# The expert stage's gated sum: rows weighed before they are stored, and added in memory by the store

## The chip, the cores and the metric

The kernel runs on one core of a Trainium2 chip. The metric is device time in microseconds (us) of that core; less is better. Before the change it is 2638.87 us, the median of three runs (2636.39 to 2640.18).

## The reference

Two transformer blocks on 1024 tokens of 1024 features. The change touches the last part of the second block only, the mixture of experts and the last norm:

```python
def hierarchical_moe(xn, w_rg, b_rg, w_re, b_re, w1, w3, w2):
    # xt: 1024 tokens x 1024; 4 groups of 8 experts, top-1 group, top-2 experts in it
    gate = p_g * jax.nn.softmax(top_v, axis=-1)              # 2 gates a token
    expert = g_idx[:, None] * EXPERTS_PER_GROUP + top_i      # 2 experts a token
    # assignments sorted by expert, padded to blocks of MOE_BLOCK = 128 rows of one expert
    def block_ffn(args):
        tok, e = args
        xb = xt[tok]
        hb = jax.nn.silu(xb @ w1[e]) * (xb @ w3[e])          # 1024 -> 512
        return hb @ w2[e]                                    # 512 -> 1024
    y = jnp.einsum('nk,nkd->nd', gate, y_assign)             # weigh and add the two rows of a token
    return y

x = x + hierarchical_moe(rmsnorm_2(x, norm_moe_g), ...)
return rmsnorm_2(x, norm_f_g)
```

All of it is in float32. A token has two expert outputs; each is weighed by its gate and both are added to the residual row, and the row is then normalised.

## The kernel before

The stages up to the router are unchanged. The last call of `project_out` writes the residual rows (x3, 1024 rows of 4 KB in memory) and the normalised rows (xn), and computes the router's logits.

`route` (line 2260) runs mostly on VectorE (DVE). It finds the two experts and the two gates of each token (lines 2372 and 2373: an SBUF table `gates` of 128 partitions by 2 by 8) and the tables of slots. A block is 128 slots of one expert; every expert has one block (its first 128 assignments), and a 33rd block and a loop for further blocks take what is over. A slot is a partition. `slot_token` says which token a slot holds, `slot_row` says which row of the 2048 rows of y_rows its output goes to (token, plus 1024 for the second choice). Slots are filled from the first partition on; the entry of an empty slot is beyond the bounds check, and the indirect DMA leaves it out.

`experts` (line 2484) runs the 33 blocks. Every engine walks through the same list `steps()`: for block b the two halves of w1, the turned h of block b-1, the two halves of w3, the turned x of block b+1, the two halves of w2 of block b-1.

- SyncE (SP) loads the weights of block b+2 (`ExpertWeights.load`, line 2463): w1, w3 and w2 are 2 MB each, as 128 partitions of 16 KB, in two buffers each. Each load waits until DVE has finished with the raw weights of two blocks ago. SP issues in program order. Since w2 of a block is used about one block later than its w1 and w3, the load of w2 waits longest, and w1 and w3 of the next block go out right behind it: one burst of 6 MB a block.
- ScalarE (ACT) rounds each half matrix to w_hi (line 2735), DVE computes the rest w_lo (line 2796); a ring of four halves feeds TensorE (PE), which does three products for one (lines 2660, 2666, 274 to 276).
- GpSimd (POOL) issues two indirect DMAs a block: `gather_rows` (line 2435) fetches 128 rows of xn into ex_x, and `scatter` (line 2597) stores ex_y to y_rows. The first may run when x of two blocks before is turned, the second when ACT has copied the block's output out of PSUM (line 2755, ex_y<-ex_py), in two buffers.
- During the last block SP also loads the eight tiles of residual rows (line 2579).

`combine` (line 2850) begins when all scatters have landed. SP loads the eight y tiles of the first choice (line 2864), ACT the eight of the second (line 2872). For each tile of 128 tokens DVE multiplies and adds twice (2888, 2890), ACT takes the sum of squares and the root (2876, 2877), DVE the reciprocal and the norm (2896, 2897), and SP stores the tile (2867). DVE runs the adds of the next tile ahead of the norm of this one.

All DMA queues, whichever engine issues, share the same 16 DMA engines. In the profile q1 is SP's queue, q0 POOL's and q10 ACT's.

Of the kernel before, what the change touches and what calls it, by code (L numbers as in the profile page):

```python
# [27 lines left out]
P = 128  # L28
# [2231 lines left out]
def route(c, expert_weights, pl, bias, gates, slot_token, slot_row, extra_expert, n_rest, xg):  # L2260
# [7 lines left out]
    with ExitStack() as s:  # L2268
        def sb(name, shape, dt=F32):
            return s.enter_context(nc.sbuf_tensor(f"rt_{name}", shape, dt))  # L2270
# [19 lines left out]
        none, row = sb("none", [P, NBLK]), sb("row", [P, NBLK])  # L2290
        slots, filled = c.sem("rt_slots"), c.sem("rt_filled")
# [45 lines left out]
        def route_dve(dve):  # L2337
# [35 lines left out]
            step(V.tensor_tensor(gates[:, 1, :], gates[:, 0, :], v2[:, :], ALU.mult))  # L2373

# [48 lines left out]
            step(V.scalar_tensor_tensor(slot_row[:, :], pt[:, 0:NBLK], -1.0, row[:, :], ALU.add, ALU.add))  # L2423
            step(V.tensor_tensor(cmp[:, :, :], pend[:, :].unsqueeze(1).to_broadcast([P, NEXTRA, NE]),
# [6 lines left out]
        return route_sp, route_pool, route_pe, route_act, route_dve  # L2431
# [52 lines left out]
def experts(c, weights, xn, y_rows, slot_token, slot_row, n_rest, xg, x3, tail, gates, out, routing):  # L2484
# [32 lines left out]
    x, _, gain, x_in, gain_in = tail  # L2517
    route_sp, route_pool, route_pe, route_act, route_dve = routing
    x_t = x3.rearrange("(t p) d -> t p d", p=P)

    with ExitStack() as s:
# [7 lines left out]
        idx = sb("idx", [P, LINE], I32)  # L2529
        xT_hi, xT_lo = sb("xT_hi", [P, D], F32R), sb("xT_lo", [P, D], F32R)  # L2530
# [9 lines left out]
        combine_sp, combine_act, combine_dve = combine(c, s, tail, y_rows, gates, out, y[:, 0, :])  # L2540
# [22 lines left out]
        with nc.Block() as block:  # L2563
            @block.sync
            def _(sp):
                route_sp(sp)

                for b in range(2, NB):
                    weights.load(sp, b, up_lo, down_lo)

                def load(i):
                    e = sp.value_load(weights.extra_expert[0:1, bass.ds(i + 1, 1)], min_val=0, max_val=NE - 1)
                    sp.wait_ge(r_free, i + 1)
                    for m, w in (("w1", weights.w1), ("w3", weights.w3), ("w2", weights.w2)):
# [12 lines left out]
            def _(pool):  # L2587
                route_pool(pool)

                def gather(b):  # L2590
                    if b >= 2:
                        pool.wait_ge(x_turned, b - 1)
                    gather_rows(nc, xg, xn, slot_token, b, g_in[b % 2])

                def scatter(b):
                    pool.wait_ge(y_ready, b + 1)
                    nc.gpsimd.indirect_dma_start(y_rows, bass.IndirectOffsetOnAxis(slot_row[:, b:b + 1].bitcast(U32), 0),
                                                 y[:, b % 2, :], None, bounds_check=2 * S - 1, oob_is_err=False
                                                 ).then_inc(y_out[b % 2], 16)

                gather(0)
                gather(1)
                gather(2)
                for n, m, b, half in steps():
                    if m == "turn_x" and b + 2 < NB:
                        gather(b + 2)
                    if m == "w1" and half == 1 and b >= 2:
                        scatter(b - 2)
                scatter(NB - 2)
                scatter(NB - 1)  # L2610

                def regather(i):
                    pool.wait_ge(r_free, i + 1)
                    nc.gpsimd.tensor_copy(idx[:, 0:1], slot_token[:, bass.ds(i + NB, 1)])
                    nc.gpsimd.tensor_copy(idx[:, 1:2], slot_row[:, bass.ds(i + NB, 1)]).then_inc(r_idx, 1)
                    pool.wait_ge(r_idx, i + 1)
                    pool.sem_inc(r_gathers, 1)
                    nc.gpsimd.indirect_dma_start(xg[:, 0, :], None, xn,
                                                 bass.IndirectOffsetOnAxis(idx[:, 0:1].bitcast(U32), 0),
                                                 bounds_check=S - 1, oob_is_err=False).then_inc(r_x_in, 16)  # L2620
                    pool.wait_ge(r_y_ready, i + 1)
                    pool.sem_inc(r_gathers, 1)
                    nc.gpsimd.indirect_dma_start(y_rows, bass.IndirectOffsetOnAxis(idx[:, 1:2].bitcast(U32), 0),
                                                 y[:, 0, :], None, bounds_check=2 * S - 1, oob_is_err=False
                                                 ).then_inc(r_y_out, 16)
# [100 lines left out]
            def _(act):  # L2726
# [24 lines left out]
                def store(b, n):  # L2751
# [3 lines left out]
                    nc.scalar.activation(y[:, b % 2, :], p_y[:, :], ACT.Copy).then_inc(y_ready, 1)  # L2755
# [18 lines left out]
                def block_of_rest(i):  # L2774
# [4 lines left out]
                    nc.scalar.activation(y[:, 0, :], p_y[:, :], ACT.Copy).then_inc(r_y_ready, 1)  # L2779
# [60 lines left out]
def combine_buffers(c, weights, xg):  # L2840

    x = [w[1][:, t * D:(t + 1) * D] for w in (weights.w1s, weights.w3s) for t in range(NT // 2)]
    y = [w[0][:, t * D:(t + 1) * D] for w in (weights.w1s, weights.w3s, weights.w2s) for t in range(NT // 2)]
    y += [weights.w2s[1][:, t * D:(t + 1) * D] for t in (1, 2)] + [xg[:, t, :] for t in range(2)]
    return x, y, weights.w2s[1][:, 0:D], [c.sem(f"cb_x_in{t}") for t in range(NT)], c.sem("cb_gain_in")


def combine(c, stack, tail, y_rows, gates, out, sq):  # L2850


    nc, io = c.nc, c.io
    x, y, gain, x_in, gain_in = tail
# [3 lines left out]
    eps_ready, added, rms_ready, ready = (c.sem(f"cb_{n}") for n in ("eps", "added", "rms", "ready"))  # L2858
    y_in = [c.sem(f"cb_y_in{t}") for t in range(NT)]
    out_done = c.sem("cb_out_done")  # L2860

    def combine_sp(sp):
        for t in range(NT):
            sp.dma_start(y[2 * t], y_rows[t * P:(t + 1) * P, :]).then_inc(y_in[t], 16)
# [5 lines left out]
    def combine_act(act):  # L2870
        for t in range(NT):
            act.dma_start(y[2 * t + 1], y_rows[S + t * P:S + (t + 1) * P, :]).then_inc(y_in[t], 16)
        act.wait_ge(eps_ready, 1)
        for t in range(NT):
            act.wait_ge(added, t + 1)
# [4 lines left out]
    def combine_dve(dve):  # L2880
        nc.vector.memset(eps[:, :], EPS).then_inc(eps_ready, 1)
        dve.wait_ge(gain_in, 16)

        def add(t):
            xx = x[t]
            dve.wait_ge(x_in[t], 16)
            dve.wait_ge(y_in[t], 32)
# [5 lines left out]
        def norm(t):  # L2893
            xx = x[t]
            dve.wait_ge(rms_ready, t + 1)
            c.vstep(dve, nc.vector.reciprocal(ss[:, 2, t:t + 1], ss[:, 1, t:t + 1]))
            nc.vector.scalar_tensor_tensor(xx, xx, ss[:, 2, t:t + 1], gain, ALU.mult, ALU.mult
                                           ).then_inc(ready, 1)

        for t in range(NT):  # L2900
            add(t)
            if t >= 1:
                norm(t - 1)
        norm(NT - 1)
# [18 lines left out]
def build(nc, io):  # L2923
# [4 lines left out]
    x1, x2, x3, xn = (scratch(f"{n}_rows", S) for n in ("x1", "x2", "x3", "xn"))  # L2928
    og, yb, y_rows = scratch("og_rows", S), scratch("yb_rows", S), scratch("y_rows", 2 * S)
# [6 lines left out]
    with ExitStack() as ctx:  # L2936
# [8 lines left out]
        with ExitStack() as late:  # L2945
            with ExitStack() as front:
# [56 lines left out]
                bias = late.enter_context(nc.sbuf_tensor("rt_bias", [P, LINE], F32))[:, 0:NG + NE]  # L3003
# [8 lines left out]
            routing = route(c, expert_weights, logits, bias, gates, slot_token, slot_row, extra_expert, n_rest, xg)  # L3012
            tail = combine_buffers(c, expert_weights, xg)
            experts(c, expert_weights, xn, y_rows, slot_token, slot_row, n_rest, xg, x3, tail, gates, io["out"], routing)


# [16 lines left out]
```

## Time and profile before

| | us |
|---|---|
| median of three runs | 2638.87 |
| the profiled execution's own time | 2638.07 |
| its span, first to last instruction | 2636.3 |
| PE busy | 2483.1 (94%) |
| DVE busy | 1255.8 (48%) |
| ACT busy | 1140.5 (43%) |
| POOL busy | 598.1 (23%) |
| DMA moved | 434.78 MB, 165 GB/s on average |

The busy shares are averages over stages with quite different loads. The page also cuts the span into 40 equal slices, a digit a slice: the busy share in tenths of each engine and, in the line DMA, of the 16 DMA engines. The expert stage is the last quarter of the span. "Landing" is the time from the issue of a DMA until its semaphore has counted it as complete. The idle time of an engine is told with the instruction whose end released it.

### The profile page before, as it was taken

The numbers are of one execution on the slowest core, as the hardware profiler recorded it, in microseconds if no ns is written. First come the engines' busy times: TensorE is split into PE (matmuls) and PEld (weight loads), VectorE is DVE, ScalarE is ACT, GpSimd is POOL, SyncE is SP. The second block draws the span as 40 slices with busy tenths as digits, with TensorE's granted clock in tenths as the row PEclk, the third lists the DMA queues.
The fourth block names the chain that finished last, engine by engine and source line by source line (L and its number), as shares of the span: only waits on it lengthen the run. The fifth ranks groups of instructions, "written<-read, shape, count | busy, mean of one in ns | idle before, by whom it ended". The sixth has DMA issues, their size and how long they took to land. (4 is left out here: it accounts for less than half of the span.)

```text
span 2636.3 us, 30070 instructions
## 1 busy us (share of the span) xinstructions
PE 2483.1 (94%) x11958; PEld 1999.5 (76%) x11958; DVE 1255.8 (48%) x1583; ACT 1140.5 (43%) x1612; POOL 598.1 (23%) x497
## 2 busy tenths in 40 slices
PE   7999998889999999999999999999987999999992
PEld 6888874447787888878887877885775888888882
DVE  6420205553304121125543853006128898888886
ACT  4212225553332122214232742235225878877883
POOL 0312302213222122332220751254110111111100
PEclk9999999999999999999999999999987999999996
DMA  4322121203311131132424732441446999999996
GB/s 171 110 66 92 48 77 52 81 9 128 120 37 60 33 117 60 56 117 69 128 64 165 279 131 81 143 160 65 132 178 255 379 382 391 393 385 383 390 363 246
DMA packets 146581, 434.78 MB, mean 165 GB/s; under 512 B 16232, under 2 KB 66632, under 8 KB 133768
## 3 DMA queue, kind: packets, MB, share of 16 engines
q1 hardware_dynamic: 95536, 374.23, 37.6%
q10 hardware_dynamic: 38120, 31.50, 3.6%
q0 software_dynamic: 12784, 27.11, 2.9%
q8 instruction: 96, 1.57, 0.2%
q14 instruction: 45, 0.37, 0.0%
HBM read 377.70 MB, written 72.91 MB: 171 GB/s over the span
## 5 line engine op out<-in xcount | busy, mean ns | idle before, releaser
L2796 DVE TENSOR_TENSOR ex_w_lo<-ex_w,ex_w_hi 128x2048 fp32r<-128x2048 f32 x198 | 447.9, 2290 | 62.0 <-ACT ex_w_hi L2735 61.2
L2735 ACT ACTIVATE ex_w_hi<-ex_w 128x2048 fp32r<-128x2048 f32 x198 | 377.0, 1916 | 20.3 <-PE ex_pb L2666 11.0
L221 POOL TENSOR_TENSOR p_w_lo<-w_raw,p_w_hi 128x512 fp32r<-128x512 f32 (+1 forms) x146 | 191.5, 1345 | 627.1 <-ACT p_w_hi L249 594.9
L221 POOL TENSOR_TENSOR p_w_lo_rest<-w_raw,p_w_hi_rest 128x512 fp32r<-128x512 f32 x88 | 118.0, 1375 | 254.4 <-ACT p_w_hi_rest L249 254.4
L846 DVE CUSTOM_DVE_ANT_0 att_sc<-att_ps_s,logc 128x128 f32<-128x128 f32 (+7 forms) x96 | 71.7, 752 | 120.8 <-PE att_ps_s L781 120.4
L274 PE MATMUL p_ps<-p_w_hi,hT_hi 128*128 128x512 f32 (+1 forms) x320 | 120.9, 378 | 0.0
L276 PE MATMUL p_ps<-p_w_hi,hT_lo 128*128 128x512 f32 (+1 forms) x320 | 118.5, 370 | 0.0
L275 PE MATMUL p_ps<-p_w_lo,hT_hi 128*128 128x512 f32 (+1 forms) x320 | 118.0, 369 | 0.0
L249 ACT ACTIVATE p_w_hi<-w_raw 128x512 fp32r<-128x512 f32 (+1 forms) x133 | 74.7, 600 | 88.9 <-PE mix_ps_rest L276 49.3
L2435 POOL DMA_INDIRECT ex_x<-xn_rows,slot_token x33 | 35.5, 1075 | 338.1 <-PE ex_px L2640 315.7
L274 PE MATMUL ex_py<-ex_w_hi,ex_hT_hi 128*128 128x512 f32 x264 | 105.6, 400 | 1.9 <-DVE ex_hT_lo L2805 1.9
L274 PE MATMUL o_ps<-o_w_hi,o_m_hi 128*128 128x512 f32 x256 | 102.1, 399 | 5.0 <-DVE split_cols L1165 5.0
L2660 PE MATMUL ex_pa<-ex_w_hi,ex_xT_hi 128*128 128x512 f32 x264 | 103.9, 394 | 2.4 <-ACT ex_xT_hi L2739 1.2
L2660 PE MATMUL ex_pb<-ex_w_hi,ex_xT_hi 128*128 128x512 f32 x264 | 105.8, 401 | 0.0
L2660 PE MATMUL ex_pa<-ex_w_lo,ex_xT_hi 128*128 128x512 f32 x264 | 103.6, 392 | 0.0
L2660 PE MATMUL ex_pb<-ex_w_lo,ex_xT_hi 128*128 128x512 f32 x264 | 103.3, 391 | 0.0
L276 PE MATMUL ex_py<-ex_w_hi,ex_hT_lo 128*128 128x512 f32 x264 | 103.1, 391 | 0.0
L275 PE MATMUL ex_py<-ex_w_lo,ex_hT_hi 128*128 128x512 f32 x264 | 103.0, 390 | 0.0
L276 PE MATMUL o_ps<-o_w_hi,split_cols 128*128 128x512 f32 x256 | 101.1, 395 | 0.0
L275 PE MATMUL o_ps<-o_w_lo,o_m_hi 128*128 128x512 f32 x256 | 101.0, 395 | 0.0
L1053 POOL TENSOR_TENSOR split_cols<-plain_cols,o_m_hi 128x1024 fp32r<-128x1024 f32 x20 | 48.0, 2401 | 195.6 <-ACT o_m_hi L1116 195.6
L274 PE MATMUL p_ps<-hT_hi,p_w_hi 128*128 128x512 f32 x224 | 87.3, 390 | 0.2 <-POOL p_w_lo L221 0.2
(507 smaller groups left out, 6249.2 us busy)
## 6 DMA issues: line engine op xcount, KB each, us to landing
ex_w<-w SPq DMA_DIRECT2D x99, 2048.0 KB, 14.4
w_raw<-w_in SPq DMA_DIRECT2D x42, 1024.0 KB, 5.1
w_raw<-w_out SPq DMA_DIRECT2D x8, 1024.0 KB, 8.2
x_rows<-o_x SPq DMA_DIRECT2D x16, 512.0 KB, 2.6
qk_columns<-ml_qk_first ACTq DMA_DIRECT2D x16, 512.0 KB, 3.2
w_raw<-w_xkv SPq DMA_DIRECT2D x8, 1024.0 KB, 6.1
plain_cols<-x SPq DMA_DIRECT2D x8, 512.0 KB, 8.7
w_raw<-w_in SPq DMA_DIRECT2D x16, 256.0 KB, 4.0
```

Of the source, the lines that this page charges most:

```text
L221: emit(self.lo(n)[:, 0:w], self.half(n // (KC // 2), w)[:, n % (KC // 2), :], self.hi(n)[:, 0:w].bitcast(F32), ALU.subtract).then_inc(self ...
L249: copy = lambda out, in_: self.c.nc.scalar.activation(out, in_, ACT.Copy)
L274: pe.matmul(out, a, x, start=start, stop=False)
L275: pe.matmul(out, a, y, start=False, stop=False)
L276: return pe.matmul(out, b, x, start=False, stop=stop)
L846: nc.vector.tensor_tensor_reduce(row_of(i, k), bank_of(i, k), logc[:, S - (a + 1) * P:S], -SCALE, -NEG, ALU.add, ALU.min, nmx[:, 2 * i + k ...
L1053: nc.gpsimd.tensor_tensor(tile(cols, t), tile(plain, t), m_hi[:, t % 2, :, :].bitcast(F32), ALU.subtract).then_inc(rest, 1)
L2435: nc.gpsimd.indirect_dma_start(xg[:, b % 2, :], None, xn, bass.IndirectOffsetOnAxis(slot_token[:, b:b + 1].bitcast(U32), 0), bounds_check= ...
L2660: pe.matmul(ps[:, :], xT_hi[:, k * P:(k + 1) * P], w[:, n % RING, at], start=(k == 0 and w is w_hi), stop=False)
L2735: nc.scalar.activation(w_hi[:, n % RING, :], raw_half(n), ACT.Copy).then_inc(hi_done, 1)
L2796: nc.vector.tensor_tensor(w_lo[:, n % RING, :], raw_half(n), w_hi[:, n % RING, :].bitcast(F32), ALU.subtract).then_inc(down_lo if m == "w2 ...
```

## The change

The two weighed outputs of a token are no longer stored apart and combined at the end. The residual rows and the result of the experts share one memory tensor `sums` of 1024 + 128 rows (`x3` is its first 1024 rows). In each block ACT multiplies the output rows by the slots' gates while it copies them out of PSUM, and the scatter adds them to the rows of `sums` in memory (`compute_op=ALU.add`). For that:

- SP writes the gates once to a memory table `gate_rows` of 2048 words, and POOL gathers the 128 gates of each block from it by an indirect DMA of one word a slot, with `slot_row` as index.
- a new table `slot_sum` holds the row of `sums` for each slot: the token, or for an empty slot a spare row of its own partition, 1024 + p. So the scatter now has 128 valid rows always. Two DVE instructions more in `route` make it, and one makes `spare_row`.
- a scatter waits until the scatter before it has landed, since both may add to the same row.
- `combine` loads eight tiles of `sums`, four by SP and four by ACT, and has the norm alone; DVE's adds, the sixteen y loads and the eight x loads in the last block are gone.

```diff
 (route)
+            V.tensor_scalar(spare_row[:, :], c.const("tokid")[:, 0:1], float(S), None, ALU.add).then_inc(gates_ready, 1)
...
+            step(V.scalar_tensor_tensor(row[:, :], pt[:, 0:NBLK], -1.0, none[:, :], ALU.add, ALU.add))
+            V.tensor_scalar(slot_sum[:, 0:NBLK], row[:, :], spare_row[:, :], None, ALU.min).then_inc(rows_known, 1)
 (experts, SP)
                 route_sp(sp)
+                sp.wait_ge(gates_ready, 1)
+                with nc.allow_non_contiguous_dma(reason="one gate a token, once"):
+                    sp.dma_start(gate_rows.rearrange("(k t p) o -> p (k t) o", k=2, p=P),
+                                 gates[:, :, :].rearrange("p k t -> p (k t)").unsqueeze(2)).then_inc(gates_out, 16)
...
-                for t in range(NT):
-                    sp.wait_ge(up_lo, 4 * NE - (2 if t < NT // 2 else 0))
-                    sp.dma_start(x[t], x_t[t]).then_inc(x_in[t], 16)
 (experts, POOL)
+                def gather_gates(b):
+                    if b == 0:
+                        pool.wait_ge(gates_out, 16)
+                        pool.wait_ge(rows_known, 1)
+                    if b >= 2:
+                        pool.wait_ge(y_ready, b - 1)
+                    nc.gpsimd.indirect_dma_start(slot_gate[:, b % 2:b % 2 + 1], None, gate_rows,
+                                                 bass.IndirectOffsetOnAxis(slot_row[:, b:b + 1].bitcast(U32), 0),
+                                                 bounds_check=2 * S - 1, oob_is_err=False).then_inc(gate_in[b % 2], 16)
                 def scatter(b):
                     pool.wait_ge(y_ready, b + 1)
-                    nc.gpsimd.indirect_dma_start(y_rows, bass.IndirectOffsetOnAxis(slot_row[:, b:b + 1].bitcast(U32), 0),
-                                                 y[:, b % 2, :], None, bounds_check=2 * S - 1, oob_is_err=False
-                                                 ).then_inc(y_out[b % 2], 16)
+                    if b >= 1:
+                        pool.wait_ge(y_out[(b - 1) % 2], 16 * ((b - 1) // 2 + 1))
+                    nc.gpsimd.indirect_dma_start(sums, bass.IndirectOffsetOnAxis(slot_sum[:, b:b + 1].bitcast(U32), 0),
+                                                 y[:, b % 2, :], None, bounds_check=S + P - 1, oob_is_err=True,
+                                                 compute_op=ALU.add).then_inc(y_out[b % 2], 16)
...
                         scatter(b - 2)
+                        gather_gates(b)
 (experts, ACT, store)
-                    nc.scalar.activation(y[:, b % 2, :], p_y[:, :], ACT.Copy).then_inc(y_ready, 1)
+                    act.wait_ge(gate_in[b % 2], 16 * (b // 2) + 16)
+                    nc.scalar.activation(y[:, b % 2, :], p_y[:, :], ACT.Copy, scale=slot_gate[:, b % 2:b % 2 + 1]
+                                         ).then_inc(y_ready, 1)
 (combine)
-        for t in range(NT):
-            sp.dma_start(y[2 * t], y_rows[t * P:(t + 1) * P, :]).then_inc(y_in[t], 16)
+        for t in range(0, NT, 2):
+            load(sp, t)          # x[t] <- sums[t * P:(t + 1) * P, :]
...
-        for t in range(NT):
-            act.dma_start(y[2 * t + 1], y_rows[S + t * P:S + (t + 1) * P, :]).then_inc(y_in[t], 16)
+        for t in range(1, NT, 2):
+            load(act, t)
...
-            c.vstep(dve, nc.vector.scalar_tensor_tensor(xx, y[2 * t], gates[:, 0, t:t + 1], xx,
-                                                        ALU.mult, ALU.add))
-            nc.vector.scalar_tensor_tensor(xx, y[2 * t + 1], gates[:, 1, t:t + 1], xx, ALU.mult, ALU.add
-                                           ).then_inc(added, 1)
```

The loop for further blocks is changed in the same way.

POOL's order at the start of the expert stage before (ex_x is the gathered input, ex_y the output of a block):

```order
L2435 DMA ex_x<-xn_rows,slot_token 128x1024 [waits att_turned,o1_g_in]
L2435 DMA ex_x<-xn_rows,slot_token 128x1024
L2435 DMA ex_x<-xn_rows,slot_token 128x1024 [waits ex_x_turned] x3
L2597 DMA y_rows<-ex_y,slot_row 2048x1024 [waits ex_y_ready]
L2435 DMA ex_x<-xn_rows,slot_token 128x1024 [waits ex_x_turned]
L2597 DMA y_rows<-ex_y,slot_row 2048x1024 [waits ex_y_ready]
L2435 DMA ex_x<-xn_rows,slot_token 128x1024 [waits ex_x_turned]
L2597 DMA y_rows<-ex_y,slot_row 2048x1024 [waits ex_y_ready]
```

And with the change (ex_idx holds the gathered gates, rt_bias the table slot_sum):

```order
L2439 DMA ex_x<-xn_rows,slot_token 128x1024 [waits att_kept1,o1_x_in1]
L2439 DMA ex_x<-xn_rows,slot_token 128x1024
L2608 DMA ex_idx<-gate_rows,slot_row 128x1 [waits att_kept0,o2_post]
L2608 DMA ex_idx<-gate_rows,slot_row 128x1
L2439 DMA ex_x<-xn_rows,slot_token 128x1024 [waits o2_h_hi] x3
L2616 DMA sums_rows<-ex_y,rt_bias 1152x1024 [waits ex_y_ready]
L2608 DMA ex_idx<-gate_rows,slot_row 128x1 [waits ex_y_ready]
L2439 DMA ex_x<-xn_rows,slot_token 128x1024 [waits o2_h_hi]
L2616 DMA sums_rows<-ex_y,rt_bias 1152x1024 [waits ml_m_ready,ex_y_ready]
L2608 DMA ex_idx<-gate_rows,slot_row 128x1 [waits ex_y_ready]
L2439 DMA ex_x<-xn_rows,slot_token 128x1024 [waits o2_h_hi]
```

Two gate gathers stand before the third x gather, and from then on each block has three transfers: the adding scatter, the gate gather of the block two later, the x gather.

DVE's order at the end of the program before (ex_w and ex_x are the buffers of the tiles, cb_ss the sums of squares):

```order
L2881 MEMSET cb_eps 128x1
L2888 SCALAR_TENSOR_TENSOR ex_w_1<-ex_w_0,gates,ex_w_1 128x1024
L2890 SCALAR_TENSOR_TENSOR ex_w_1<-ex_w_0,gates,ex_w_1 128x1024
L2888 SCALAR_TENSOR_TENSOR ex_w_1<-ex_w_0,gates,ex_w_1 128x1024
L2890 SCALAR_TENSOR_TENSOR ex_w_1<-ex_w_0,gates,ex_w_1 128x1024
L2896 RECIPROCAL cb_ss<-cb_ss 128x1
L2897 SCALAR_TENSOR_TENSOR ex_w_1<-ex_w_1,cb_ss 128x1024
L2888 SCALAR_TENSOR_TENSOR ex_w_1<-ex_w_0,gates,ex_w_1 128x1024
L2890 SCALAR_TENSOR_TENSOR ex_w_1<-ex_w_0,gates,ex_w_1 128x1024
```

And with the change:

```order
L2913 MEMSET cb_eps 128x1
L2917 RECIPROCAL cb_ss<-cb_ss 128x1
L2918 SCALAR_TENSOR_TENSOR ex_w_0<-ex_w_0,cb_ss,ex_w_1 128x1024
L2917 RECIPROCAL cb_ss<-cb_ss 128x1
L2918 SCALAR_TENSOR_TENSOR ex_w_0<-ex_w_0,cb_ss,ex_w_1 128x1024
```

The two multiply-and-add instructions of each tile are gone, and reciprocal and norm follow each other tile by tile.

## Rows read from the trace of the kernel before

**Rows 1.** The page: span, engines and the span in 40 slices.
```profile
span 2636.3 us, 30070 instructions
...
PE   7999998889999999999999999999987999999992
...
DMA  4322121203311131132424732441446999999996
```

**Rows 2.** Windows of 100 us in the expert stage: busy us of each engine.
```profile
core 0: us, PE busy (x) PEld busy (x) DVE busy (x) ACT busy (x) POOL busy (x), PEclk, DMA share, GB/s
...
2200.00:2300.00 100.00, 100.00 (x475) 83.83 (x474) 89.79 (x52) 80.32 (x57) 12.26 (x11) 1.00 0.96 389
2300.00:2400.00 100.00, 100.00 (x473) 83.81 (x472) 89.27 (x51) 80.74 (x57) 11.58 (x11) 1.00 0.96 393
```

**Rows 3.** The chain of waits, one expert block: start us, us, what.
```profile
2123.02 1.81 PE ex_pa L2660 x8
...
2140.77 1.81 PE ex_pa L2660 x8
```

**Rows 4.** Weight loads: who waited for line 2474 and its landing; 2477's landing; line 2481.
```profile
  ACT ex_w_hi L2735: 4.9, 6
...
DMA to landing us min/median/max: 8.2/14.4/16.3
...
DMA to landing us min/median/max: 7.8/19.5/21.3
...
L2481 SPq DMA_DIRECT2D ex_w<-w x33: 327/328/529, 1968.7 to 2559.8; - x33
...
DMA to landing us min/median/max: 7.7/8.7/22.5
```

**Rows 5.** Fine windows around the next burst's issue, columns as in rows 2.
```profile
2208.23:2210.01 1.78, 1.78 (x9) 1.50 (x8) 1.62 (x2) 1.78 (x2) 0.00 (x0) 1.00 1.05 433
...
2222.25:2223.00 0.75, 0.75 (x5) 0.62 (x4) 0.73 (x2) 0.22 (x1) 0.00 (x0) 1.00 0.49 208
```

**Rows 6.** DMA queues between 2060 and 2540 us: packets, MB, share of 16 engines.
```profile
DMA packets 19523, 185.06 MB, mean 386 GB/s; under 512 B 5626, under 2 KB 5626, under 8 KB 9092
...
q1 hardware_dynamic: 11703, 170.50, 87.0%
q0 software_dynamic: 7795, 14.21, 7.7%
```

**Rows 7.** Idle of ACT before line 2755 (us, times); line 2597's durations, starts and landing.
```profile
  PE ex_py L276: 33.1, 33
...
L2597 POOL DMA_INDIRECT y_rows<-ex_y,slot_row x33: 974/1009/1291, 2036.1 to 2593.6; - x33
...
DMA to landing us min/median/max: 2.6/10.9/12.1
```

**Rows 8.** Timeline of the start: start us, us, instruction, idle before it.
```profile
1993.00 0.21 DVE L2423 SCALAR_TENSOR_TENSOR slot_row<-rt_pt,rt_row 128x48 int32<-128x48 f32 x1
...
2000.95 1.00 POOL L2435 DMA_INDIRECT ex_x<-xn_rows,slot_token  x1 [4.75 <-PE ex_px L2640]
```

**Rows 9.** Timeline of the end, columns as in rows 8.
```profile
2596.28 3.57 SPq L2864 DMA_DIRECT2D ex_w<-y_rows  x7
...
2601.16 1.28 DVE L2888 SCALAR_TENSOR_TENSOR ex_w<-ex_w,gates,ex_w 128x1024 f32<-128x1024 f32 x1 [12.13 <-DMA ex_w<-y_rows]
...
2603.86 1.06 ACT L2876 ACTIVATE ex_y<-ex_w 128x1024 f32<-128x1024 f32 x1 [11.02 <-DVE ex_w L2890]
...
2606.85 1.28 DVE L2897 SCALAR_TENSOR_TENSOR ex_w<-ex_w,cb_ss 128x1024 f32<-128x1024 f32 x1
2607.62 0.19 ACT L2876 ACTIVATION_READ_ACCUMULATOR ex_y<-ex_w 128x1 f32 x1
2607.84 0.29 ACT L2877 ACTIVATE cb_ss<-cb_ss,cb_eps 128x1 f32<-128x1 f32 x1
...
2631.94 1.28 DVE L2897 SCALAR_TENSOR_TENSOR ex_w<-ex_w,cb_ss 128x1024 f32<-128x1024 f32 x1
```

More of the change, by code:

```diff
@@ L2257, in load_router, with route @@
     sp.dma_start(bias[:, NG:], io["b_re_2"].partition_broadcast(P)).then_inc(w_in, 16)
-def route(c, expert_weights, pl, bias, gates, slot_token, slot_row, extra_expert, n_rest, xg):
+def route(c, expert_weights, pl, bias, gates, slot_token, slot_row, slot_sum, extra_expert, n_rest, xg):
     nc = c.nc
@@ L2481, in load, with experts @@
             sp.dma_start(self.w2s[j][:, :], self.w2[at].rearrange("e p n -> (e p) n")).then_inc(self.w2_in[j], 16)
-def experts(c, weights, xn, y_rows, slot_token, slot_row, n_rest, xg, x3, tail, gates, out, routing):
+def experts(c, weights, xn, sums, gate_rows, slot_token, slot_row, slot_sum, n_rest, xg, tail, gates, out, routing):
     nc = c.nc
@@ L2516, in experts @@
     pieces = {n: (m, b, half) for n, m, b, half in steps() if n is not None}
-    x, _, gain, x_in, gain_in = tail
-    route_sp, route_pool, route_pe, route_act, route_dve = routing
-    x_t = x3.rearrange("(t p) d -> t p d", p=P)
+    _, gain, _, gain_in = tail
+    (route_sp, route_pool, route_pe, route_act, route_dve), gates_ready, rows_known = routing
     with ExitStack() as s:
@@ L2529, in experts @@
         idx = sb("idx", [P, LINE], I32)
+        slot_gate = idx[:, 8:8 + 3].bitcast(F32)
         xT_hi, xT_lo = sb("xT_hi", [P, D], F32R), sb("xT_lo", [P, D], F32R)
@@ L2539, in experts @@
         y_out, g_in, all_stored = [c.sem(f"ex_y_out{j}") for j in range(2)], [c.sem(f"ex_g_in{j}") for j in range(2)], c.sem("ex_all_stored")
-        combine_sp, combine_act, combine_dve = combine(c, s, tail, y_rows, gates, out, y[:, 0, :])
+        gate_in, gates_out = [c.sem(f"ex_gate_in{j}") for j in range(2)], c.sem("ex_gates_out")
+        r_gate_in = c.sem("ex_rest_gate_in")
+        combine_sp, combine_act, combine_dve = combine(c, s, tail, sums, out, y[:, 0, :])
         x_turned, x_hi, x_lo = c.sem("ex_x_turned"), c.sem("ex_x_hi"), c.sem("ex_x_lo")
@@ L2620, in regather @@
                                                  bounds_check=S - 1, oob_is_err=False).then_inc(r_x_in, 16)
+                    nc.gpsimd.indirect_dma_start(slot_gate[:, 2:3], None, gate_rows,
+                                                 bass.IndirectOffsetOnAxis(idx[:, 1:2].bitcast(U32), 0),
+                                                 bounds_check=2 * S - 1, oob_is_err=False).then_inc(r_gate_in, 16)
                     pool.wait_ge(r_y_ready, i + 1)
                     pool.sem_inc(r_gathers, 1)
-                    nc.gpsimd.indirect_dma_start(y_rows, bass.IndirectOffsetOnAxis(idx[:, 1:2].bitcast(U32), 0),
-                                                 y[:, 0, :], None, bounds_check=2 * S - 1, oob_is_err=False
-                                                 ).then_inc(r_y_out, 16)
+                    for j in range(2):
+                        pool.wait_ge(y_out[j], 16 * ((NB + 1 - j) // 2))
+                    nc.gpsimd.indirect_dma_start(sums, bass.IndirectOffsetOnAxis(idx[:, 2:3].bitcast(U32), 0),
+                                                 y[:, 0, :], None, bounds_check=S + P - 1, oob_is_err=True,
+                                                 compute_op=ALU.add).then_inc(r_y_out, 16)
                 over_rest(pool, regather)
@@ L2778, in block_of_rest @@
                     act.wait_ge(y_out[0], 16 * ((NB + 1) // 2))
-                    nc.scalar.activation(y[:, 0, :], p_y[:, :], ACT.Copy).then_inc(r_y_ready, 1)
+                    act.wait_ge(r_gate_in, 16 * i + 16)
+                    nc.scalar.activation(y[:, 0, :], p_y[:, :], ACT.Copy, scale=slot_gate[:, 2:3]).then_inc(r_y_ready, 1)
                     act.wait_ge(r_y_out, 16 * i + 16)
@@ L2837, in _, with combine_buffers, combine @@
                 combine_dve(dve)
[L2840 to L2854, printed above, removed]
+def combine_buffers(c, weights):
+    x = [w[0][:, t * D:(t + 1) * D] for w in (weights.w1s, weights.w3s) for t in range(NT // 2)]
+    return x, weights.w2s[1][:, 0:D], [c.sem(f"cb_x_in{t}") for t in range(NT)], c.sem("cb_gain_in")
+def combine(c, stack, tail, sums, out, sq):
+    nc = c.nc
+    x, gain, x_in, gain_in = tail
     out_t = out.rearrange("(t p) d -> t p d", p=P)
@@ L2857, in combine, with load @@
     eps = stack.enter_context(nc.sbuf_tensor("cb_eps", [P, 1], F32))
-    eps_ready, added, rms_ready, ready = (c.sem(f"cb_{n}") for n in ("eps", "added", "rms", "ready"))
-    y_in = [c.sem(f"cb_y_in{t}") for t in range(NT)]
+    eps_ready, rms_ready, ready = (c.sem(f"cb_{n}") for n in ("eps", "rms", "ready"))
     out_done = c.sem("cb_out_done")
+    def load(engine, t):
+        engine.dma_start(x[t], sums[t * P:(t + 1) * P, :]).then_inc(x_in[t], 16)
     def combine_sp(sp):
-        for t in range(NT):
-            sp.dma_start(y[2 * t], y_rows[t * P:(t + 1) * P, :]).then_inc(y_in[t], 16)
+        for t in range(0, NT, 2):
+            load(sp, t)
         for t in range(NT):
@@ L2882, in combine_dve @@
         dve.wait_ge(gain_in, 16)
[L2884 to L2887, printed above, removed]
-            c.vstep(dve, nc.vector.scalar_tensor_tensor(xx, y[2 * t], gates[:, 0, t:t + 1], xx,
-                                                        ALU.mult, ALU.add))
-            nc.vector.scalar_tensor_tensor(xx, y[2 * t + 1], gates[:, 1, t:t + 1], xx, ALU.mult, ALU.add
-                                           ).then_inc(added, 1)
-        def norm(t):
-            xx = x[t]
+        for t in range(NT):
             dve.wait_ge(rms_ready, t + 1)
             c.vstep(dve, nc.vector.reciprocal(ss[:, 2, t:t + 1], ss[:, 1, t:t + 1]))
[L2897 to L2904, printed above, removed]
+            nc.vector.scalar_tensor_tensor(x[t], x[t], ss[:, 2, t:t + 1], gain, ALU.mult, ALU.mult).then_inc(ready, 1)
     return combine_sp, combine_act, combine_dve
@@ L3011, in build @@
             xg = late.enter_context(nc.sbuf_tensor("ex_x", [P, 2, D], F32))
-            routing = route(c, expert_weights, logits, bias, gates, slot_token, slot_row, extra_expert, n_rest, xg)
-            tail = combine_buffers(c, expert_weights, xg)
-            experts(c, expert_weights, xn, y_rows, slot_token, slot_row, n_rest, xg, x3, tail, gates, io["out"], routing)
+            routing = route(c, expert_weights, logits, bias, gates, slot_token, slot_row, slot_sum, extra_expert, n_rest, xg)
+            tail = combine_buffers(c, expert_weights)
+            experts(c, expert_weights, xn, sums, gate_rows, slot_token, slot_row, slot_sum, n_rest, xg, tail, gates,
+                    io["out"], routing)
 def kernel(**inputs):
```

19 lines of the change are left out of this document (13 added, 6 removed).

## The prediction

> **What bounds the kernel now.** I read the page first: the profiled execution spans 2636.3 us, and in the slices behind about 2043 us, the 32nd on (the expert stage, which the change rewrites), PE and DMA both stand at 9 tenths [rows 1]. So two resources are nearly full there and the first question is which has room. The windows view of that stage gives PE 100.00 of 100 us at full clock, ACT 80, DVE 89, POOL 12, and the DMA engines 0.94 to 0.96 at 381 to 393 GB/s [rows 2]. The chain of waits is PE alone, and the same matmul of ex_pa starts at 2123.02 and again at 2140.77: one expert block takes 17.75 us, set by PE [rows 3]. Then the DMA side of the same block, from the issues of the three 2 MB weight loads: w2 (line 2481) lands 8.7 us after issue, w1 (2474) 14.4, w3 (2477) 19.5, by the median [rows 4]. The three are issued within a microsecond of each other once a block, and 19.5 is more than 17.75: the slowest DMA engine still works on w3 when the next three are issued. ACT already waits for w1 six times, 4.9 us together [rows 4]. DMA is thus the second bound, right behind PE.
>
> Why 0.95 and not 1.00, if the last load is late? In a fine window at the moment of the next burst (2222.5 us) the DMA share is 0.49, where it is 1.05 in the middle of a burst [rows 5]. About half of the 16 engines have run dry and the other half has not. I choose this reading: each gather and each scatter handles 128 slots, of which 3469 rows in 54 transfers, 64 on average, carry a token (row count: 14.21 MB by 4096 bytes; 7795 packets are 54 times 144) [rows 6]. The live slots are the first ones of a block, so the first partitions, and about eight engines would carry all of them. The empty slots are skipped.
>
> **Prices of DMA work.** In 480 us queue q1 moved 170.50 MB in 87.0% of 16 engines' time: 25.5 GB/s an engine, so a 16 KB weight row is 0.64 us; 24 of them per engine and block (3 times 128 rows over 16) are 15.4 us. Queue q0 took 7.7%, 591 us of engine time for 3469 rows: 0.17 us a row, its tiny packets included [rows 6]. At a good rate in a slice, 433 GB/s [rows 5], the same are 0.605 and 0.151 us, and 24 weight rows 14.5 us. An engine with eight live rows in each of gather and scatter has 15.4 + 2.7 = 18.1 us of work by the first price and 14.5 + 2.4 = 16.9 by the second, against a block of 17.75: full or nearly.
>
> **The change, part by part.**
> - The weighted rows now come from ACT's copy with a scale per partition (the same rows and columns as before, and ACT is idle 20% of the stage [rows 2] and 33.1 us in front of this very instruction [rows 7]: hidden, even at twice the time). POOL issues a third indirect transfer per block, the gate gather, at the 1.0 us of the scatter's row; POOL is 12% busy. The gate lands a block before it is used. Both cost nothing. Its up to 128 packets of 4 bytes are not in the trace as reads; from below 0, from above a full row price each (8 times 0.17 = 1.4 us an engine); nearest are q0's 5626 packets under 512 B, which are so cheap that 64 real rows and 80 of them together cost only 0.17 us a row [rows 6]. I take 0.1 us a block.
> - The scatter now always writes 128 rows, since an empty slot adds to a spare row behind the tokens: 8 rows on every engine. For an engine that already had eight this is nothing, for the others 8 times 0.17 = 1.4 us of room that they have (the 0.49 share).
> - Each row is added, not stored: the engine must read the old 4 KB beside the new. No row shows an accumulate. From below, it costs no more than a plain row (the read hides behind the write): 0 per block. It can't be a gain, as the bytes only grow. From above the trace gives no end; I price one more row read at 0.151 to 0.17 us, so 8 rows add 1.2 to 1.4 us to every engine. I take this one, twice the plain row, since the nearest row, a 4 KB gather out of memory, costs 0.17 for exactly such a read, and the engines have no idle time to hide it in.
> - Sum per block: 14.5 + 1.2 + 2.4 + 0.1 = 18.2 at the best rates, 15.4 + 1.4 + 2.7 + 0.1 = 19.6 at the mean ones. Before, the mean prices gave 18.1 where 17.75 was met, so they are some 0.35 too high: 19.2. Over 17.75 this is 0.5 to 1.5 us. I take 1.2. The bursts with scatters beside them run from 2036 us (the first scatter) to 2560 (the last weight load) [rows 4, 7]: 524 by 17.75 = 30 blocks, rounded: 30 times 1.2 = 36 us. PE then waits for ACT, and ACT for the weights.
> - Each scatter now waits until the one before has landed. That was 10.9 us by the median and the scatters are 17.75 apart [rows 7]; with twice the turns on each ring perhaps 15. Still hidden. Behind it on POOL stand the gate gather and the next x gather, whose rows are used most of a block later.
> - Start: three small table instructions on DVE, 0.2 us each by line 2423's row [rows 8], one of them in front of the first gather; and the write of the gates (2048 words), 128 packets an engine, which share the rings with the first gather, between 0 and 1 us. The first two gate gathers fit into the 4.75 us that POOL is idle before the third gather [rows 8]. I take 0.5 us.
> - Tail. Before: last scatter issued 2593.6, landed 2.6 us later at 2596.2; y loads from 2596.28; first add 2601.16; first norm 2606.85, last 2631.94, so 3.6 us a tile on average (two adds and a norm of 1.28 each); end 2636.3 [rows 1, 7, 9]. The eight x loads in the last block go too, and give nothing: the chain there is PE's. Now: the last scatter lands 1.3 us later (8 more row reads), loads at 2597.6. First Square at +4.9 (as the first pair before), 2602.5. From Square to the end of the first norm it was 2603.86 to 2608.13, 4.3 us with the table load: 2606.8. Then ACT sets the pace, a tile from its Square to its root's end, 1.06, 0.19 and 0.29 with little overlap, 1.5 us (DVE's norm of 1.28 and a reciprocal, about the same); 7 more tiles end at 2617.3. The store of the last tile takes the 3.1 us from the last norm's end (2633.2) to the end of the span: 2620.4. The 4 MB of loads need 10 us at 410 GB/s, before tile 7 is due; with the stores 8.4 MB or 20 us, about even with this pace; +1 for that. Gain: 2636.3 - 2621.4 = 15.
> Sum: +36 + 0.5 - 15 = +21.5: span 2658, and the execution's own time 2638.07 + 21.5 = 2659.6. The median of the three runs, 2638.87, is 0.8 above the profiled one, so 2660.
>
> The Trainium skill has a rule against this change: "Collectives: The Full Stack", the section on the bandwidth ceiling, says that a reduce in the DMA engines is slowed not by the addition but by reading two sources, so it runs at about half of a copy (a measured ratio of 1.93). No run here shows an accumulate yet. With 1.93 in place of 2, the eight rows would add 1.2 us instead of 1.3, and the sum stands.
>
> **Rivals.**
> A. The read of the old row is hidden; an accumulated row costs as a stored one. Then the fullest engine gains 0.1 us a block, 3 us over 30, the last scatter lands as before, the tail gives 16: 3 + 0.5 - 16 = -12.5, time 2626. For it: reading and writing are two sides of an engine and a plain store uses each once; the half of the engines without live rows has room. Against it: the share of 0.95, the late w3. This is the faster side; it decides at 0.5 us a block (30 times 0.5 = 15).
> B. The forecast, twice the row: 2660. With the lower price (0.5 a block) 2639, with the upper (1.5) 2669.
> C. Each row is slower still, because the add runs slower than the stream or each row waits for its own read: three times a plain row is 8 times 0.17 more, 1.4 us a block or 41 us on top of B: about 2700, and open upwards. For it: nothing in the trace; against it: nothing either.
> D. The serial wait: if the accumulate lands after more than 17.75 us, POOL holds the next x gather and PE starves. It needs 7 us more than the 10.9 of before. Price: the excess per block; at 20 us 30 times 2.2 = 66 us, about 2690.
>
> **Chances.** B 52%, A 28%, C 14%, D 6%. B's own range is 2639 to 2672. The range to hold 8 in 10 takes A in and half of C: 2620 to 2697. A measurement of this kernel tells about 0.2% (5 us) from no change. Faster: A nearly whole and the cheap edge of B, 0.31. Within 0.2%: the low end of B, 0.07. Slower: 0.62.
>
> **What would show it.** For B: PE's period in blocks 2 to 31 goes from 17.75 to about 18.9; ACT's waits for ex_w from 4.9 us to tens; the DMA share flat near 1.0 with no dip before the burst; q0 bytes up; w3's landing over 20 us. For A: the period stays 17.75 to 17.85. For C the period is over 20. For D the waits of POOL for its own transfers. The tail from the last scatter to the end should shrink from 43 to about 28 us in all cases. I'm wrong if the period does not move although the accumulated rows' share of q0 doubles, which would mean that the engines had the room.

## The result and the profile after

The changed kernel takes 2650.36 us (median of four runs, 2647.93 to 2655.01), against 2637.63 us of the kernel before in the runs beside it: ratio 1.0049, 95% interval 1.0038 to 1.0061. It is slower by 12.7 us, or 0.5%. The profiled execution took 2650.05 us. The forecast was 2660.

The page, span and slices of PE and DMA, against [rows 1]:

```profile
span 2648.1 us, 30136 instructions
...
PE   7999998889999999999999999999977999999994
...
DMA  4323121203311031233325633351546999999996
```

The span grew by 11.8 us. The windows of the expert stage (columns as in [rows 2]):

```profile
core 0: us, PE busy (x) PEld busy (x) DVE busy (x) ACT busy (x) POOL busy (x), PEclk, DMA share, GB/s
...
2200.00:2300.00 100.00, 96.60 (x447) 78.79 (x446) 85.44 (x50) 74.45 (x54) 24.85 (x15) 1.00 1.01 385
2300.00:2400.00 100.00, 98.08 (x462) 80.94 (x462) 86.58 (x50) 75.95 (x55) 28.59 (x17) 1.00 1.01 388
```

PE is now idle for 3.4 and 1.9 us in 100, and it runs 447 and 462 matmuls where it ran 475 and 473. ACT fell from 80 us to between 74 and 76, POOL doubled, and the DMA share rose from between 0.94 and 0.96 to 1.01. The share adds up the time of packets, and since it can pass 1, packets of one engine overlap a little. It is a sign that the engines are full, but no proof that they set the pace: in e1 and e4 below it is 0.99 while PE is never idle. The proof that the other bound has taken over is in the waits. These are the weight loads of w1 (line 2478), w3 (2481) and w2 (2485), with who waited for them (us, times), against [rows 4]:

```profile
  ACT ex_w_hi L2763: 68.7, 29
...
DMA to landing us min/median/max: 12.7/17.8/18.6
...
  ACT ex_w_hi L2763: 64.6, 29
...
DMA to landing us min/median/max: 7.4/24.2/24.9
...
L2485 SPq DMA_DIRECT2D ex_w<-w x33: 327/328/507, 1968.4 to 2586.7; - x33
...
DMA to landing us min/median/max: 8.1/12.4/24.6
```

w3 lands 24.2 us after issue, before the change 19.5. ACT waits for w1 and w3, 29 times each; before the change it waited six times, for w1 alone. The waits in order:

```profile
ACT ex_w_hi L2763 <- DMA ex_w<-w: 133.3, 58, 3.1
DVE ex_w_lo L2827 <- ACT ex_w_hi L2763: 87.3, 96, 2.0
...
PE ex_pa L2688 <- DVE ex_w_lo L2827: 13.1, 22, 0.9
```

So DMA holds up ACT, ACT holds up DVE, DVE holds up PE, though by far the most of ACT's 133 us is absorbed by its slack (the 30 blocks became 23.3 us longer). The period comes from the loads of w2: the first burst with all buffers in use was issued at 2030.8 us, the last w2 at 2586.7 (line 2485 above), 30 periods of 18.53 us on average. Before the change it was 2027.2 to 2559.8, a period of 17.75.

The chain of waits near the end (start us, us, what) now contains the weight loads, which it did not in [rows 3], and shows the tail, to be set against [rows 9]:

```profile
2475.85 18.37 DMA ex_w<-w
2494.24 1.93 ACT ex_w_hi L2763
...
2618.08 6.38 DMA sums_rows<-ex_y,rt_bias
2624.54 4.47 DMA ex_w<-sums_rows
2629.10 1.15 ACT ex_y L2908 x2
...
2632.16 1.28 DVE ex_w L2918
2633.55 1.28 DVE ex_w L2918
...
2641.91 1.28 DVE ex_w L2918
```

The tail has no adds: eight norms, 1.39 us apart. The span in pieces, us:

| from | to | before | after | difference |
|---|---|---|---|---|
| start of the span | slot_row is made (line 2423, now 2425) | 1993.0 | 1992.9 | -0.1 |
| slot_row | first full burst | 34.2 | 37.9 | +3.7 |
| first full burst | last w2 issued, 30 blocks | 532.6 | 555.9 | +23.3 |
| last w2 issued | last scatter issued | 33.8 | 31.4 | -2.4 |
| last scatter issued | end | 42.7 | 30.0 | -12.7 |

### The profile page after: what moved, and what is told of

It reads as the page before. It is cut to its first block and busy times, and to the rows that moved or that the text cites. A ratio compares the mean times of both kernels' runs of the same rounds, so it can differ in the third digit from the quotient of the medians.

```text
span 2648.1 us, 30136 instructions
## 1 busy us (share of the span) xinstructions
PE 2488.1 (94%) x11958; PEld 1994.8 (75%) x11958; DVE 1235.4 (47%) x1570; ACT 1130.6 (43%) x1612; POOL 693.3 (26%) x530
## 2 busy tenths in 40 slices
DMA packets 147397, 435.32 MB, mean 164 GB/s; under 512 B 16920, under 2 KB 67320, under 8 KB 134584
## 5 line engine op out<-in xcount | busy, mean ns | idle before, releaser
L2616 POOL DMA_INDIRECT sums_rows<-ex_y,rt_bias x33 | 64.2, 1944 | 296.4 <-ACT ex_y L2784 286.6
```

The source lines that it names most:

```text
L2616: nc.gpsimd.indirect_dma_start(sums, bass.IndirectOffsetOnAxis(slot_sum[:, b:b + 1].bitcast(U32), 0), y[:, b % 2, :], None, bounds_check=S ...
```

## Experiments

**e1: stored, not added.**

```diff
-                 y[:, b % 2, :], None, bounds_check=S + P - 1, oob_is_err=True, compute_op=ALU.add)
+                 y[:, b % 2, :], None, bounds_check=S + P - 1, oob_is_err=True)
```

> The kernel after, but its 33 scatters store their 128 rows instead of adding them (so the sum over experts is left out of the result); everything else stays, the serial wait and the gate gather too. Theory (an added row costs a DMA engine twice a stored one, 0.34 us for 0.17): the engines lose 8 x 0.17 = 1.3 us of work a block, 18.5 becomes 17.2, PE's 17.75 sets the period again, and the time falls by about 30 x 0.78 = 23 us plus 1 to 2 us for the last scatter: about 2625. Rival (the three indirect transfers a block and their serial wait cost the time, not the addition): the period stays above 18.2 and the time at 2645 or more.

Measured: 2627.36 us, ratio to the kernel before 0.9957 (0.9940 to 0.9974). DMA queues between 2060 and 2540 us, the w2 loads, and the last scatter in the chain of e1, then the queues of the kernel after:

```profile
q1 hardware_dynamic: 11682, 170.15, 87.2%
q0 software_dynamic: 8659, 21.19, 11.2%
...
L2485 SPq DMA_DIRECT2D ex_w<-w x33: 327/328/530, 1971.6 to 2567.4; - x33
...
2603.03 3.34 DMA sums_rows<-ex_y,rt_bias
```

```profile
DMA packets 19463, 182.98 MB, mean 381 GB/s; under 512 B 4567, under 2 KB 4567, under 8 KB 9535
...
q1 hardware_dynamic: 11147, 162.27, 82.7%
q0 software_dynamic: 8292, 20.37, 18.3%
...
sums_rows<-ex_y,rt_bias POOLq DMA_INDIRECT x25
```

The period is 17.75 (2034.8, the first full burst, to 2567.4). So of all that the change adds to a block, it is the addition that costs the 23 us; the serial wait and the gate gather, which e1 keeps, cost nothing beside PE. The price of a row follows from the queue shares. In e1, 11.2% of 480 us and 16 engines is 860 us for 5173 rows (21.19 MB by 4096 bytes): 0.166 us a row, stored or gathered. In the kernel after, 18.3% is 1405 us for 4973 rows; the window holds the rows of 26 scatters (25 issued in it, and one just before it), which are 3328, and the other 1645, gathered, take 273 us at e1's price; 1132 us by 3328 is 0.34 us an added row. That is 2.05 times a stored one. The records of single packets in the same window say it directly. By the median a 4 KB packet takes 0.159 us in e1, whether it is gathered or stored; in the kernel after there are two groups, one at 0.159 and one at 0.328, the added rows. A 16 KB weight packet takes 0.611 us in both. The bytes counted do not show it: 20.37 MB, one count a row. The rule cited from the Trainium skill in the prediction ("Collectives: The Full Stack", the section on the bandwidth ceiling, ratio 1.93) agrees with this.

**e2: empty slots left out of the addition. e3: slots spread over the partitions. e4: both.**

```diff
 e2, e4
-            V.tensor_scalar(slot_sum[:, 0:NBLK], row[:, :], spare_row[:, :], None, ALU.min)
+            V.tensor_copy(slot_sum[:, 0:NBLK], row[:, :])       # and oob_is_err=False in the scatters
 e3, e4 (the constant from which the place of a slot is made)
-    c["iota"][:] = p[None, :]
+    c["iota"][:] = (p // 2 + P // 2 * (p % 2))[None, :]
```

> The kernel after, with empty slots left out of the adding scatter as they were before (index beyond the bounds check): 64 rows added a block on average, not 128. Theory of the prediction (the live rows lie in the first partitions, and the same eight or so engines carry them all): those engines still have eight added rows, the period stays near 18.5, the time near 2650. Rival (rows are spread over all engines): 64 rows less at 0.34 us over 16 engines are 1.3 us a block, the period is 17.75 and the time about 2626.

> The kernel after, with the slots of a block permuted: rank r goes to partition 2r (r under 64) or 2(r-64)+1, so that the live rows lie in every group of partitions. The scatter has 128 rows anyway, so only the x gather changes. If the gather's live rows were all on eight engines, these lose 0.6 us a block and the period falls from 18.5 to about 18.0 (time about 2636); if the gather was even already, nothing moves: 2650.

> Both: slots permuted and empty slots left out of the adding scatter. Every engine has four added rows (1.3 us) and four gathered ones (0.7 us) beside 15.4 us of weights: 17.4 us, under PE's 17.75. Both theories of where the live rows lie expect the period 17.75 here, and about 2650 - 23 - 1 = 2626. If it stays near 2650, the cost is not in the DMA engines' rows at all.

Measured: e2 2649.26 us (ratio 1.0046, 1.0032 to 1.0061), e3 2633.98 (0.9983, 0.9974 to 0.9993), e4 2628.65 (0.9963, 0.9948 to 0.9977). First e2, its queues, w2 loads and a window over the stage:

```profile
q1 hardware_dynamic: 11143, 162.35, 83.3%
q0 software_dynamic: 8299, 14.00, 11.7%
...
L2485 SPq DMA_DIRECT2D ex_w<-w x33: 327/328/1012, 1970.2 to 2589.7; - x33
...
2100.00:2500.00 400.00, 388.88 (x1810) 318.66 (x1809) 337.94 (x194) 297.90 (x216) 108.55 (x65) 1.00 0.95 367
```

Its q0 moves a third fewer bytes than the kernel after and takes 11.7% and not 18.3% of the engines' time, yet its period is 18.54 (2033.6 to 2589.7), the same as with all 128 rows added. So the added rows that e2 leaves out were not on the engines that set the pace. The mean share of all DMA traffic is 0.95 here, lower than e4's 0.99 below, and yet e2's PE waits and e4's does not: the mean over 16 engines is no measure of the fullest one. Then the w2 loads of e3 and e4, each with a window over the stage (columns as in [rows 2]):

```profile
L2485 SPq DMA_DIRECT2D ex_w<-w x33: 327/328/508, 1969.3 to 2571.3; - x33
...
2100.00:2500.00 400.00, 398.71 (x1881) 332.05 (x1880) 350.88 (x201) 310.38 (x223) 113.27 (x67) 1.00 1.02 394
```

```profile
L2485 SPq DMA_DIRECT2D ex_w<-w x33: 327/328/1027, 1970.8 to 2564.8; - x33
...
2100.00:2500.00 400.00, 400.00 (x1895) 335.41 (x1895) 358.51 (x204) 321.32 (x225) 110.34 (x67) 1.00 0.99 386
...
  ACT ex_w_hi L2763: 1.3, 1
```

e3's first full burst was at 2031.7: period 17.99. e4's was at 2032.2: 17.75, PE full, one wait of ACT for w1. e2 and e4 differ by nothing but the partitions in which the live rows lie, and by 20.6 us. So the live rows of a block did lie on some of the engines only, those of the scatter (e2 against the kernel after: half of the added rows gone, and the period stays) and those of the gather (e3 against the kernel after, 0.54 us a block). e4 also keeps the serial wait of the scatters: that wait costs nothing (rival D).

These periods are means of 30, and they contain a start in which the loads are still ahead: the first two periods of the kernel after and the first eight of e3 are 17.75 us, the rest 18.59 and 18.07 on average.

**e5: the gates' write late.**

```diff
                 sp.wait_ge(gates_ready, 1)
+                sp.wait_ge(g_in[0], 16)
...
-                gather_gates(0)
-                gather_gates(1)
                 gather(2)
+                gather_gates(0)
+                gather_gates(1)
```

> The kernel after, with the write of the gates to memory held back until the first x gather has landed, and the first two gate gathers put behind the third x gather. Theory (the 2048 single words of the gates' write, landing 19.9 us after issue, hold up the first x gather, which landed 8.3 us after issue and not 4.4, on the chain): the first turned x is 3.7 us earlier and the time falls from 2650 to about 2646. Rival (the 3.7 us come from elsewhere, or the late write holds up the second or third gather by as much): no change, 2650.

Measured: 2647.23 us, ratio to the kernel before 1.0032 (1.0020 to 1.0044), beside 1.0049 of the kernel after; the intervals overlap, so the trace decides. Timeline of the start, first of the kernel after (and the landing of line 2575), then of e5:

```profile
1979.14 0.38 SPq L2575 DMA_DIRECT2D gate_rows<-gates  x1
...
1992.85 0.21 DVE L2425 SCALAR_TENSOR_TENSOR slot_row<-rt_pt,rt_row 128x48 int32<-128x48 f32 x1
...
1993.64 1.51 POOL L2439 DMA_INDIRECT ex_x<-xn_rows,slot_token  x1 [22.28 <-DVE slot_token L2422]
...
2001.96 1.97 PE L2668 MATMUL ex_px<-const_small,ex_x 128*128 128x128 f32 x8 [9.74 <-DMA ex_x<-xn_rows,slot_token]
...
DMA to landing us min/median/max: 19.9/19.9/19.9
```

```profile
1994.34 0.21 DVE L2425 SCALAR_TENSOR_TENSOR slot_row<-rt_pt,rt_row 128x48 int32<-128x48 f32 x1
...
1999.75 1.97 PE L2669 MATMUL ex_px<-const_small,ex_x 128*128 128x128 f32 x8 [6.04 <-DMA ex_x<-xn_rows,slot_token]
1999.77 0.38 SPq L2576 DMA_DIRECT2D gate_rows<-gates  x1
```

In the kernel after, the first turn of x starts 8.3 us after its gather was issued (1993.64), in e5 4.6 us after (issued 1995.13); before the change it was 4.4 (1993.79 to 1998.21). From slot_row to the first full burst it is 34.6 us in e5 (1994.34 to 2028.9), 37.9 in the kernel after, 34.2 before. So the early write of the gates did cost the 3.7 us. (e5 moves the first gate gathers too, but in the kernel after the first of them is issued only at 1999.8, when the x gather is already late.) How it does so is less plain. The write lands 19.9 us after its issue, at 1999.0. These are windows of the kernel after, first while the words of the write are under way and then around the issue of the x gather (1993.64), then one of the kernel before, from 1.2 us after its gather's issue:

```profile
1990.00:1992.00 2.00, 2.00 (x11) 2.00 (x10) 0.32 (x1) 0.00 (x0) 0.00 (x0) 0.50 0.58 28
1992.00:1997.00 5.00, 0.22 (x2) 0.05 (x1) 4.43 (x12) 0.00 (x0) 2.53 (x2) 0.50 0.06 0
```

```profile
1995.00:1998.00 3.00, 0.00 (x0) 0.00 (x0) 2.93 (x4) 0.00 (x0) 1.01 (x1) 0.50 0.55 135
```

The engines are not busy with the words when the gather is issued: from 1992 to 1997 their share is 0.06, and nothing moves. A 4-byte packet of the write takes 0.009 us by the median, and an engine has 128 of them, 1.2 us. The write is still not complete for 6 us more, and the gather's rows do not move either. e5 shows the same with the load that follows the write there (line 2478, issued 1.8 us after the write):

```profile
2002.50:2012.00 9.50, 9.08 (x32) 7.38 (x33) 7.92 (x4) 6.30 (x6) 0.98 (x1) 0.78 0.54 40
...
DMA to landing us min/median/max: 16.6/16.6/16.6
```

All queues together move 40 GB/s for 9.5 us, and this load lands after 16.6 us where it took 8.2 before the change. In e5 that costs little: the stretch to the first full burst is 34.6 us and before the change 34.2. What holds up the transfers behind the 2048 words, once their packets have passed, no run here shows.

**e6: spread, empty slots left out, gates late, all three.**

> Slots spread over the partitions, empty slots left out of the adding scatter, and the gates' write late: the three together. The period is PE's 17.75 as in e4, and the start gives 3.7 us if the theory of e5 holds: about 2628.5 - 3.7 = 2625. If the start's loss was something else: 2628.5.

Measured: 2623.95 us, ratio 0.9948 (0.9935 to 0.9962): the fastest of all, 13.7 us under the kernel before by the ratio, and it leaves nothing of the reference out. Its period is 17.75 (2023.4 to 2556.0). Its interval overlaps that of e4. The profiles also differ by up to 7.6 us in when slot_row is made, which the change hardly touches (1988.4 in e6, 1996.0 in e1), so they are best compared from there to the end: 643.3 us before, 655.2 in the kernel after, 631.9 in e4, 629.6 in e6. The late write gives 2.3 of the 3.7 us expected.

**e7: e3 with the gate gather for two blocks only.**

```diff
                         scatter(b - 2)
-                        gather_gates(b)
...
-                    act.wait_ge(gate_in[b % 2], 16 * (b // 2) + 16)
+                    act.wait_ge(gate_in[b % 2], 16)
```

> The kernel of e3 (slots spread, 128 rows added, DMA engines the bound at a period of 17.99), with the gate gather done for the first two blocks only and their gates used for all blocks (the result is weighed wrongly). It prices the gate gather where the DMA engines bind. Theory (0.1 us a block or less): period 17.89 or more, time 3 us lower at most, 2631 to 2634. Rival (its words cost as rows do, 8 x 0.17 us): the period falls to 17.75 and the time by 7 us, 2627.

Measured: 2635.23 us (ratio 0.9987, 0.9978 to 0.9997), e3's 0.9983. A window of its stage:

```profile
2100.00:2500.00 400.00, 398.57 (x1880) 331.60 (x1879) 350.57 (x200) 309.31 (x222) 75.11 (x45) 1.00 1.02 394
```

PE has the same 398.6 of 400 us as in e3 (398.7) and the period is 17.97 (2031.2 to 2570.4) beside 17.99. The gate gather costs 0.02 us a block by this pair, nothing that can be told from zero, though it adds an instruction of 1.9 us to POOL. One reason can be counted: without 31 of these gathers the kernel has 146406 packets and not 147397, so one has 32 packets, half of them with the words, eight in a packet. The gates' write has about 2048 of one word each.

**e8: the kernel before with spread slots.**

> The kernel before with the slots spread over the partitions. Theory (the fullest DMA engines carried eight gathered and eight stored rows beside 14.7 us of weights, 17.2 us in a block of 17.75): they lose four and four, 1.3 us; ACT's six waits for weights (4.9 us) go, the dip before each burst is shallower, but PE sets the period, so the time stays within 0.1% of before (2638). Rival (the DMA engines cost the kernel before something too): it gets faster by more than 5 us.

Measured: 2639.43 us, ratio 1.0001 (0.9992 to 1.0010): no change. The fine windows before a burst, and w3's landing, against [rows 4, 5]:

```profile
2219.25:2220.00 0.75, 0.75 (x5) 0.62 (x4) 0.72 (x2) 0.68 (x1) 0.00 (x0) 1.00 0.68 279
2220.00:2220.75 0.75, 0.75 (x6) 0.65 (x5) 0.75 (x1) 0.00 (x0) 0.00 (x0) 1.00 0.18 71
...
DMA to landing us min/median/max: 7.6/18.5/19.7
```

The share falls to 0.18 where it fell to 0.49 before: now nearly all engines run dry before the next burst, w3 lands after 18.5 and not 19.5 us, and ACT no longer waits for weights at all. PE's period of 17.75 stays, so this room had no value for the kernel before. It is what the added rows of e4 and e6 live on.

## Why the prediction was right, and where its sizes were off

- The mechanism, B, is shown: an added row takes twice a stored one, the DMA engines pass PE as the bound, and the block gets longer. A falls by the price of 0.34 us (e1 against the kernel after), C by the same number. D falls by e4, which keeps the wait, and by the landing of the scatters, 14.1 us at most in e7 and never 17.75.
- The reading that the live rows sit on part of the engines, chosen from the dip to 0.49, is shown by e2, e3, e4 and e8. That it is eight of them was not counted, and the period doesn't need it: one engine with eight live rows in every transfer is enough.
- The step that was off is a size. The term of 1.2 us a block was too large: 0.78 was met. The sum at the best rates gave 18.2, the one at the mean prices 19.2 after correction; 18.53 lies nearer to the first. The mean price of a weight row, 0.64 us, is pulled up by some packets that take longer; the median packet takes 0.611. The mean prices had already given 18.1 for a block that took 17.75; I corrected for this only in part. With the medians of single packets, 0.611 us a weight row, 0.159 a plain and 0.328 an added one, an engine with eight rows of each kind has 14.7 + 1.3 + 2.6 = 18.6 us (18.53 met, and 18.59 behind the start). One with four gathered and eight added rows has 17.9 (e3, 17.99, and 18.07 behind the start), and before the change it is 17.2, under PE's 17.75. These prices were read after the result and forecast nothing. Over 30 blocks 36 us were forecast and 23.3 measured.
- The last block gave 2.4 us back, not in the sum: with no further loads behind them, the last weights land early and PE catches up on what it waited. This part is argued from the table; no run was made for it.
- The start was put at 0.5 us and is 3.7. The bound "up to 1 us" for the gates' write was wrong. I priced the engines' time for 128 packets, and that was about right (1.2 us). What was missing is the time for which the transfers behind them stand still. e5 shows that the write is the cause, not how it works.
- The prediction gives q0 5626 packets under 512 B. That is the count of all queues; q0 has 4329 of them, so its 80 a transfer stand, and with them the price of a row. It also counted up to 128 packets for a gate gather, and there are 32. Neither changes its sum.
- The tail was forecast to give 15 us and gives 12.7. The last scatter takes 6.4 us to land, not 3.9. Storing 128 rows already takes 3.3 (e1), where the scatter before the change, with fewer live rows, took 2.6. POOL's instruction takes 1.56 us and not 0.99, another 0.6, and the eight added rows an engine 1.3. Of the 1.1 us left I know only where they lie: the first 26 rows take 0.49 to 1.28 us each, the later ones mostly 0.328. The pace is 1.39 us a tile, not 1.5. From the start of the last norm to the end it takes 6.2 us, before 4.4: the stores come every 1.39 us and fill the engines (share 1.02 from 2637 to 2643 us), and one lands 5.0 us after issue by the median, before 3.4.
- Together: 12.7 us too much for the blocks and 2.4 for the last one, 5.5 too little for start and tail: the span grew by 11.8 and not 21.5 us. That the total came within 10 us is in part luck, since errors of 15.1 and 5.5 us had opposite signs.

## What to carry to other kernels

An indirect DMA that adds costs its DMA engine two rows for one. Beside a load stream that nearly fills the engines, what exceeds the room of the fullest engine is paid: here eight added rows brought 1.3 us more work, and the block grew by 0.78. Look at the fullest engine, not at the mean share. If part of a 128-row transfer is left out, spread the rows that remain over the partitions: here this is one constant, and with the empty slots left out it turned a loss of 0.5% (e2) into a gain of 0.4% (e4); with the gates written late the gain is 0.5% (e6). Write a table of single words to memory at a time when nothing waits for a DMA. Whether a few long runs would do better was not tried.

## What the runs showed of the hardware

- An adding row of 4 KB: 0.34 us of an engine by the queue's share and 0.328 by single packets, a stored or gathered one 0.17 and 0.159 (e1, kernel after). POOL's instruction takes 1.56 to 2.02 us for a scatter that adds 128 rows (kernel after) and 1.03 by the median for one that stores them (e1).
- The same number of live rows, gathered and added, costs 18.54 us a block in the first partitions; spread out, it fits under PE's 17.75 (e2, e4).
- 2048 single words from SBUF to memory took 1.2 us of each engine, but landed 6 us (kernel after) and 9 us (e5) behind their packets, and what was issued behind them stood still: an x gather came 3.7 us later (kernel after), a 2 MB load landed after 16.6 and not 8.2 us (e5). 128 single words gathered cost nothing that could be measured (e7).
